# A row tile's projection in two halves of the tokens at the end of a two-layer network

## What is computed

```python
h2 = rmsnorm_2(x, norm2_g[l]) * (1.0 + scale2) + shift2
u = causal_dwconv(h2 @ w_up[l], ffn_conv_w[l], ffn_conv_b[l])
u_gate, u_val = u[..., :D_FF_2], u[..., D_FF_2:]
x = x + gate2 * ((jax.nn.silu(u_gate) * u_val) @ w_down[l])
return rmsnorm_2(x, final_g)

def rmsnorm_2(x, g):
    y = xf * lax.rsqrt(jnp.mean(xf * xf, axis=-1, keepdims=True) + EPS)
    return y * g
```

## Time and profile before

| | |
|---|---|
| median of 3 runs | 1795.24 us (1795.19 to 1796.18) |
| the profiled execution | 1792.66 us |
| its span, first to last instruction | 1790.9 us |
| PE busy | 1775.9 us, 99% of the span |
| PEld, DVE, ACT, POOL busy | 1421.8, 1041.1, 789.2, 268.5 us |
| DMA | 202.06 MB, 113 GB/s in the mean |

### The profile page before, as it was taken

The page is one execution under the profiler, slowest core; times in us unless marked ns, Lnnn a source line. Parts: engine busy times, 40 slices in busy tenths (PEclk is TensorE's granted clock), DMA queues, the critical chain, the costliest instruction groups (busy, mean ns, idle before and its releaser), DMA issues.

```text
span 1790.9 us, 20963 instructions
## 1 busy us (share of the span) xinstructions
PE 1775.9 (99%) x8086; PEld 1421.8 (79%) x8086; DVE 1041.1 (58%) x1675; ACT 789.2 (44%) x1248; POOL 268.5 (15%) x349
## 2 busy tenths in 40 slices
PE   9999999999999999999999999999999999999998
PEld 7888888878887888888887678777778788888887
DVE  8864554756566544554478796256544765435543
ACT  6554544524344222222264666356653444224443
POOL 4766536300000000000001110322210000000000
PEclk9999999999999999999999999999999999999999
DMA  6222223134344534554341422421143233233321
GB/s 218 96 87 89 71 89 92 53 114 152 94 147 164 188 141 178 209 189 153 118 135 58 132 92 76 144 66 59 36 164 95 83 94 95 94 94 94 95 94 71
DMA packets 65411, 202.06 MB, mean 113 GB/s; under 512 B 7520, under 2 KB 11872, under 8 KB 65312
## 3 DMA queue, kind: packets, MB, share of 16 engines
q1 hardware_dynamic: 65312, 200.72, 33.8%
HBM read 192.30 MB, written 8.40 MB: 112 GB/s over the span
## 4 chain that ended last, share of the span: by engine, by line
PE 94%; DVE 2%; ACT 2%; issue 0%; DMA 0%; SPq 0%; POOL 0%; ACTq 0%; DVEq 0%; POOLq 0%
PE bank L258 28%; PE bank L260 28%; PE bank L259 28%; PE bank L659 2%; PE bank L687 1%; PE bank L672 1%; PE bank L304 1%; PE bank L356 1%; PE bank L341 1%; DVE wlo L1446 1%; PE bank L537 1%; ACT whi L856 1%; PE bank L386 0%; PE bank L377 0%; PE bank L300 0%
## 5 line engine op out<-in xcount | busy, mean ns | idle before, releaser
L258 PE MATMUL bank<-tiler,whi 128*128 128x512 f32 x2260 | 912.8, 404 | 4.2 <-DVE wlo L1446 2.3
L260 PE MATMUL bank<-tiler,wlo 128*128 128x512 f32 x2260 | 892.9, 395 | 0.0
L259 PE MATMUL bank<-tiler,whi 128*128 128x512 f32 x2260 | 892.6, 395 | 0.0
L856 ACT ACTIVATE whi<-raw 128x1024 fp32r<-128x1024 f32 x284 | 298.8, 1054 | 511.6 <-PE bank L260 502.9
L258 PEld LDWEIGHTS bank<-tiler,whi 128*128 128x128 f32 x2260 | 427.1, 189 | 117.0 <-issue 16.6
L260 PEld LDWEIGHTS bank<-tiler,wlo 128*128 128x128 f32 x2260 | 426.4, 189 | 99.5
L259 PEld LDWEIGHTS bank<-tiler,whi 128*128 128x128 f32 x2260 | 426.9, 189 | 96.2 <-issue 1.7
L1446 DVE TENSOR_TENSOR wlo<-raw,whi 128x1024 fp32r<-128x1024 f32 x263 | 326.7, 1246 | 264.7 <-ACT whi L856 264.4
L2279 POOL TENSOR_TENSOR stat<-stat,scl 128x4 f32<-128x4 f32 x7 | 7.5, 1080 | 748.9 <-DVE stat L1954 428.2
L2270 POOL TENSOR_TENSOR wlo<-raw,whi 128x1024 fp32r<-128x1024 f32 x21 | 49.9, 2378 | 209.5 <-ACT whi L856 209.5
L2218 DVE SCALAR_TENSOR_TENSOR tile<-bank,sm,tile 128x511 f32<-128x511 f32 x42 | 31.5, 750 | 85.8 <-ACT tile L1410 54.1
(11 more groups left out here) (381 smaller groups left out, 1576.2 us busy)
## 6 DMA issues: line engine op xcount, KB each, us to landing
raw<-wst SPq DMA_DIRECT2D x284, 512.0 KB, 3.6
wide<-wadaT SPq DMA_DIRECT2D x52, 512.0 KB, 3.3
tile<-xT SPq DMA_DIRECT2D x16, 256.0 KB, 6.1
spare<-tile SPq DMA_DIRECT2D x16, 256.0 KB, 2.2
tile<-spare SPq DMA_DIRECT2D x16, 256.0 KB, 5.6
out<-tile SPq DMA_DIRECT2D x8, 256.0 KB, 2.5
tile<-gblk SPq DMA_DIRECT2D x5, 256.0 KB, 4.7
us<-tile SPq DMA_DIRECT2D x4, 256.0 KB, 2.0
```

Of the source, the lines that this page charges most:

```text
L258: e.matmul(bank, whi[:, o:o + 128], hi, start=start, stop=False)
L259: e.matmul(bank, whi[:, o:o + 128], lo, start=False, stop=False)
L260: e.matmul(bank, wlo[:, o:o + 128], hi, start=False, stop=stop).then_inc(*sig("blk", n))
L856: e.activation(whi[:, c % NHL * W:(c % NHL + 1) * W], raw[:, c % NRAW * W:(c % NRAW + 1) * W], ACT.Copy).then_inc(*sig("hi", c))
```

## The change

The down projection's row tile 7 of the second part is taken out of the loops. Its 11 blocks are gone through twice, first for tokens 0 to 255 (t = 0, in the bank it had), then for tokens 256 to 511 (t = 1, in bank 7), by matmuls of 256 columns. Both passes use the same blocks, so the weights' stream is the same. For each half DVE adds to the residual (`hd7`), makes the copy times the gain (`gs7`, which ACT did before), and later inverts the root and scales two banks; ACT squares, takes the root and scales two banks. Between the blocks of the second pass stand the transposes whose inputs are there and the sums of the first half. The transposed banks of j = 3 move to banks 3 and 7. The stores' order becomes 0, 4, 1, 5, 2, 6, 3, 7. Steps of chunks on ACT and DVE keep their places: the step for row tile 7 still stands behind row tile 6's on ACT.

```diff
@@ program
+        def out_bank(half_, j):
+            return B[(7 if half_ else 3) if j == 3 else j if half_ else 4 + j]
@@ tensor
-                for m in range(2, 8):
+                for m in range(2, 8 - hf):
                     proj("dn", (hf, m), bank2(p + m, "h_dn", hf, m), ACTS2, k0=11 * hf)
                 p += 8
+            n0, last_bank = count[0], bank2(p - 1, "hd7", 1)
+            count[0] += 11
+
+            def last(t, ks):
+                to = (B[7] if t else last_bank)[:, 256 * t:256 * t + 256]
+                for k in ks:
+                    n = n0 + k
+                    if t == 0:
+                        if n % CB == 0:
+                            e.wait_ge(*lo_at(n // CB))
+                        blocks[n:n + 1] = [("dn", 11 + k, 7)]
+                        first.setdefault(("dn", (1, 7)), n)
+                    o = n // CB % NHL * W + n % CB * 128
+                    hi, lo = (R(x)[:, 256 * t:256 * t + 256] for x in ACTS2[k])
+                    e.matmul(to, whi[:, o:o + 128], hi, start=k == 0, stop=False, skip_group_check=True)
+                    e.matmul(to, whi[:, o:o + 128], lo, start=False, stop=False, skip_group_check=True)
+                    ins = e.matmul(to, wlo[:, o:o + 128], hi, start=False, stop=k == 10, skip_group_check=True)
+                    if k == 10:
+                        ins.then_inc(*sig("dn7", t))
+
...
+            def half_total(t, bank):
+                e.wait_ge(*at("acc", "fin", 6))
+                for x in range(2):
+                    e.matmul(bank[:, x:x + 1], F(64)[:, 256 * t + 128 * x:256 * t + 128 * x + 128], ones[:, 0:1], start=x == 0,
+                             stop=False, skip_group_check=True)
+                e.wait_ge(*at("sq", "fin", 7, t))
+                for x in range(2):
+                    ins = e.matmul(bank[:, x:x + 1], F(66)[:, 256 * t + 128 * x:256 * t + 128 * x + 128], ones[:, 0:1],
+                                   start=False, stop=True, skip_group_check=True)
+                ins.then_inc(*sig("tot", "fin", t))
...
-            e.wait_ge(*at("h_dn", 1, 4))
-            total2("fin", 64, sums_at)
-            out_turn(0, range(4), [0, 1])
-            total3("fin", 66, sums_at)
-            out_turn(0, range(4), [2, 3])
-            out_turn(1, range(4), [4, 5, 6, 7])
...
+            def out_turn(half_, j, ms):
+                if half_ and ms[0] == 4:
+                    if j < 3:
                         e.wait_ge(*at("h_dn", 1, 4 + j))
-                        if j == 0:
-                            e.wait_ge(*at("root", "fin"))
-                    for m in ms:
+                    else:
+                        e.wait_ge(*at("hd7", 1))
+                elif j == 3:
+                    e.wait_ge(*at("hd7", 0))
+                for m in ms:
+                    if m < 7:
...
+                    else:
+                        e.wait_ge(*at("gs7", j // 2))
+                    ins = e.transpose(out_bank(half_, j)[:, m % 4 * 128:m % 4 * 128 + 128],
+                                      F(OG[m])[:, j * 128:(j + 1) * 128], ident[:, :])
+                if ms[-1] % 4 == 3:
+                    ins.then_inc(*sig("otr", half_, j))
+
+            last(0, range(11))
+            last(1, [0, 1])
+            out_turn(0, 0, [0, 1, 2, 3])
+            out_turn(0, 1, [0, 1, 2, 3])
+            last(1, [2, 3])
+            out_turn(1, 0, [4, 5, 6])
+            out_turn(1, 1, [4, 5, 6])
+            last(1, [4])
+            half_total(0, B[6])
+            last(1, [5, 6])
+            out_turn(1, 0, [7])
+            out_turn(1, 1, [7])
+            out_turn(0, 3, [0, 1, 2, 3])
+            last(1, [7, 8])
+            e.wait_ge(*at("root", "fin", 0))
+            out_turn(0, 2, [0, 1, 2, 3])
+            last(1, [9, 10])
+            out_turn(1, 2, [4, 5, 6])
+            e.wait_ge(*at("fin", 0))
+            half_total(1, B[4])
+            out_turn(1, 3, [4, 5, 6])
+            out_turn(1, 2, [7])
+            out_turn(1, 3, [7])
@@ scalar
+            e.wait_ge(*at("acc", "fin", 5))
+            for t in range(2):
+                cols = slice(256 * t, 256 * t + 256)
+                e.wait_ge(*at("hd7", t))
+                e.activation(F(66)[:, cols], F(HS[7])[:, cols], ACT.Square).then_inc(*sig("sq", "fin", 7, t))
+                e.wait_ge(*at("tot", "fin", t))
+                e.activation(stat[:, ST_F + 2 * t:ST_F + 2 * t + 2], B[4 if t else 6][:, 0:2], ACT.Sqrt, scale=1.0 / 1024,
+                             bias=scl[:, HALF + 1:HALF + 2]).then_inc(*sig("root", "fin", t))
+                e.wait_ge(*at("inv", "fin", t))
+                for j in (2 * t, 2 * t + 1):
+                    e.wait_ge(*at("otr", 1, j))
+                    e.activation(F(OT[4 + j]), out_bank(1, j), ACT.Copy, scale=stat[:, ST_F + j:ST_F + j + 1]).then_inc(
+                        *sig("fin_a", j))
@@ vector
+            for t in range(2):
+                cols = slice(256 * t, 256 * t + 256)
+                e.wait_ge(*at("dn7", t))
+                e.scalar_tensor_tensor(out=F(HS[7])[:, cols], in0=(B[7] if t else B[(p - 1) % 4])[:, cols], scalar=mod[:, 47:48],
+                                       in1=F(HS[7])[:, cols], op0=MUL, op1=ADD).then_inc(*sig("hd7", t))
+                e.wait_ge(*at("hd7", t))
+                e.tensor_scalar(F(OG[7])[:, cols], F(HS[7])[:, cols], col("gf2", 7), None, MUL).then_inc(*sig("gs7", t))
+                root_at = stat[:, ST_F + 2 * t:ST_F + 2 * t + 2]
+                e.wait_ge(*at("root", "fin", t))
+                e.reciprocal(root_at, root_at).then_inc(*sig("inv", "fin", t))
+                e.wait_ge(*at("inv", "fin", t))
+                for j in (2 * t, 2 * t + 1):
+                    e.wait_ge(*at("otr", 0, j))
+                    e.tensor_scalar(F(OT[j]), out_bank(0, j), stat[:, ST_F + j:ST_F + j + 1], None, MUL).then_inc(*sig("fin", j))
@@ sync
-            for k in (0, 1, 4, 2, 5, 3, 6, 7):
+            for k in (0, 4, 1, 5, 2, 6, 3, 7):
```

More of the change, by code:

```diff
@@ L57 @@
         "angles": "lo_a ang ang1 ang2 rel wts lru_a mod pow bpad masks",
-        "residual": "h_out h_fd h_pg h_o2 h_dn x2 inv fin",
+        "residual": "h_out h_fd h_pg h_o2 h_dn x2 inv fin hd7 gs7",
         "gated": "ap ga_ev mg fu_ev pr_ev mg2_ev mg2 ua",
@@ L821, in tensor @@
                     proj("dn", (hf, 1), bb, ACTS2, [k], 11 * hf)
-                for m in range(2, 8):
+                for m in range(2, 8 - hf):
                     proj("dn", (hf, m), bank2(p + m, "h_dn", hf, m), ACTS2, k0=11 * hf)
                 p += 8
-            def out_turn(half_, js, ms):
-                for j in js:
-                    if half_ and ms[0] == 4:
-                        e.wait_ge(*at("h_dn", 1, 4 + j))
-                        if j == 0:
-                            e.wait_ge(*at("root", "fin"))
-                    for m in ms:
-                        e.wait_ge(*at("gs", m))
[L834 to L837, removed]
@@ L839, in tensor @@
-            sums_at = B[0][:, 508:512]
-            e.wait_ge(*at("h_dn", 1, 4))
-            total2("fin", 64, sums_at)
-            out_turn(0, range(4), [0, 1])
-            total3("fin", 66, sums_at)
-            out_turn(0, range(4), [2, 3])
-            out_turn(1, range(4), [4, 5, 6, 7])
+            n0, last_bank = count[0], bank2(p - 1, "hd7", 1)
[16 more added lines that the diff above has]
+                        ins.then_inc(*sig("dn7", t))
@@ L1424, in scalar @@
                             e.activation(stat[:, 234:235], scl[:, HALF + 1:HALF + 2], ACT.Sqrt)
[L1425 to L1434, removed]
+                        if m < 7:
+                            e.wait_ge(*at("h_dn", 1, m))
+                            square("fin", m, F(HS[m]), 64, (65, 66))
+                            e.activation(F(OG[m]), F(HS[m]), ACT.Copy, scale=col("gf2", m)).then_inc(*sig("gs", m))
+            e.wait_ge(*at("acc", "fin", 5))
[11 more added lines that the diff above has]
+                        *sig("fin_a", j))
         def vector(e):
@@ L2248, in vector @@
                         add_up("fin", m - 1, 64, (65, 66))
-                    e.wait_ge(*made("dn", (hf, m)))
-                    e.scalar_tensor_tensor(out=F(HS[m]), in0=B[(p + m) % 4], scalar=mod[:, 40 + m:41 + m], in1=F(HS[m]), op0=MUL,
-                                           op1=ADD).then_inc(*sig("h_dn", hf, m))
+                    if not hf or m < 7:
+                        e.wait_ge(*made("dn", (hf, m)))
+                        e.scalar_tensor_tensor(out=F(HS[m]), in0=B[(p + m) % 4], scalar=mod[:, 40 + m:41 + m], in1=F(HS[m]),
+                                               op0=MUL, op1=ADD).then_inc(*sig("h_dn", hf, m))
                 p += 8
[L2253 to L2258, removed]
+            for t in range(2):
[12 more added lines that the diff above has]
+                    e.tensor_scalar(F(OT[j]), out_bank(0, j), stat[:, ST_F + j:ST_F + j + 1], None, MUL).then_inc(*sig("fin", j))
         def gpsimd(e):
```

## The result

| | before | changed |
|---|---|---|
| median of 19 runs | 1794.73 us | 1796.99 us |
| lowest to highest | 1792.3 to 1796.29 us | 1795.41 to 1801.5 us |
| ratio to before, 95% interval | | 1.0019 (1.0013 to 1.0025) |
| profiled execution, its span | 1792.66, 1790.9 us | 1798.92, 1796.9 us |

The medians lie 2.26 us apart; the ratio says 3.4 us (2.3 to 4.5), as do the averages of the same runs, 1794.29 and 1797.70. That is 0.19% slower, with an interval of 0.13 to 0.25%: the slowing is real, and the middle value lies within 0.2%, but the interval reaches beyond it.

A forecast was written before the change was run, and what follows sets the result against it. TensorE was taken to bound the kernel until the last row tile, then DMA bandwidth the stores. Costs of 0.25, 2.03 and 3.50 us less gains of 0.91 and 2.61 gave +2.26, 1797.5 us; range 1795.0 to 1800.2.

The forecast's parts named there:

- Part 1: Row tile 7 on TensorE: 33 matmuls become 66 of 256 columns at 0.12 us each, 0.25 us more.
- Part 3: Second half of row tile 7: 24 transposes and the first half's sums move ahead of the last matmul, 3.50 us more.
- C: Rival for row tile 7's matmuls: weight loads not hidden, 0.227 us a matmul, 1802.5 us, slower by 0.41%; chance 0.05.
- The hole: First half of row tile 7: TensorE waits at k = 7 for the last weight chunk, costing 2.03 us.
- Part 4: First half's sums, root, scalings and four stores run beside the second half's matmuls, hidden, with 1.4 us cover.
- Part 5: Second half's chain from last matmul to its first store: 2.97 us instead of 3.88, 0.91 gained.
- Part 6: Final stores: four instead of eight behind the second half's first issue, 4.72 us instead of 7.33, 2.61 gained.
- a sign that I had named for being wrong: Idle time of PE ended by ACT or DVE after 1780, from the second half meeting a late bank or scaling.
- The sum: Whole kernel: 5.78 us later end of row tile 7, less 0.91 and 2.61 gained, gives +2.26 us.
- A: Rival: TensorE's clock halves for 3.4 us behind the wait in row tile 7, +3.96 us, 1799.2 us; chance 0.33.
- B: Rival: the wait for the last chunk doesn't arise, 2.03 us less, +0.2, 1795.5 us; chance 0.10.

## Why the prediction was right, and where its chances were off

**The steps of Part 1 to Part 3.** Forecast from the tile's first matmul to the end of the last: 13.62 us (1771.85 to 1785.47) without the clock. Measured: 13.63 in the profile whose clock stayed full with an open hole, the same 13.63 with the dummy matmuls in it, 15.22 and 15.16 where the clock halved. The matmul of 256 columns was put at 0.12, it is 0.1205; the load is hidden, C is out. The hole was put at 2.03 us; the step across it is 1778.46 - 1776.38 = 2.08, of which 0.12 is the matmul's own, so 1.96, and the step behind it is 0.23 (to 1778.69) instead of 0.12: 2.07 in all. The two kernels with and without it differ by 13.63 - 11.52 = 2.11. It went away with the chunk's earlier step, came alone with the halved matmuls, and cost nothing in the kernel before: its cause is shown. The 3.50 us of moved work came out right as a sum (with the early chunk the last matmul starts 1786.85 - 1775.61 = 11.24 behind the first, less 65 steps of 0.1205 that is 3.41), not in its parts: six transposes take 0.57 (1783.89 to 1784.46), 0.095 each and not 0.111, while the first matmul behind each group takes 0.20, a cost that I didn't have. One reading was wrong without harm: what I called 14 matmuls in the earlier trace rows are 14 records of seven float32 matmuls, so the 0.111 is the distance of records, each with its load.

**Part 4.** The first early store was put at 1783.5, 11.65 behind the tile's first matmul; it is issued 1787.04 - 1775.44 = 11.60 behind it with the dummy matmuls at full clock, and 13.19 behind it in the changed kernel's profile. No idle time of TensorE shows between the hole and the tile's end, so the waits on the first half's root and scaling cost nothing, as forecast.

**Part 5 and Part 6.** From the end of the last matmul to the first store of the second half: 2.97 forecast, 1792.13 - 1789.19 = 2.94 measured. From that store to the end: 4.72 against 4.77. The chain of steps is the one that the prediction named: residual 1789.23, square 1789.75, root 1790.86, scaling 1791.36. After 1780 TensorE has one idle time ended by another engine, 0.36 us ahead of 1790.22, ended by the square. By its letter that is a sign that I had named for being wrong; but I had meant a late bank or a late scaling, and this is the wait for the square that Part 5 has in its chain.

**The sum.** +2.26 us was forecast, for the case of a full clock. Two profiles give the stretch for that case: the dummy matmuls 21.26, +2.21, and the held stores 24.13 less the 2.78 that holding them costs, 21.35, +2.30. The medians lie 2.26 apart too, but that agreement is luck: with the halved clock in the profile the stretch is +3.88, where A had +3.96, and the averages of the runs are 3.4 apart, so 2.26 lies just below the interval (2.3 to 4.5). The 0.51 between 1797.5 and the measured 1796.99 is the base alone: 1795.24 in the first three runs, 1794.73 in nineteen.

**The rivals.** A, the clock, happens: +3.88 measured where +3.96 stood. What was off is its chance. From two idle times in one profile, one with and one without a fall, I took 0.33; behind the open hole it fell in three of four. The same two idle times of the earlier trace rows in all twelve profiles say as much: near 1430 us it fell in ten, near 963 us in eight, 18 of 24. Their length, 1.81 to 1.94 us, doesn't tell which: the 1.93 of before had no fall, 1.94 with the early chunk had one. So what I gave as the forecast was, by these profiles, the rarer case, and A the usual one. The two are also not exclusive cases for a time: profiles of the same code fall into either, so the runs probably hold a mixture, and the ratio's 3.4 us lies between 2.2 and 3.9, nearer to A. How often the clock fell in the runs isn't shown: their mean clocks don't settle it, since the halves-only kernel and the early chunk both average 0.9979 over eleven executions, and only the first has the hole. With a fall in three of four the mean of the two cases is +3.5, 1798.7 on the base that I used. B did not occur, C is excluded by the step of 0.12, and the early stores do what they should.

**What I had not counted with** is that the part of the program ahead of the change varies by up to 4.4 us from one execution to the next (the tile's first matmul at 1771.85 before, at 1776.25 with the halves only). The median before moved from 1795.24 in the first three runs to 1794.73 in nineteen, and part of the changed kernel's spread has nothing to do with it. One piece of it is the clock again: behind the idle time near 963 us, which left the clock at 1.00 in the profile of before, it was halved in the profiles of eight of the ten experiments, as here in the kernel before with the early chunk:

```profile
965.20:968.60 3.40, 3.40 (x10) 2.62 (x9) 3.29 (x6) 0.00 (x0) 0.00 (x0) 0.50 0.00 0
```

Such a halving costs 1.65 us: from the end of this idle time to the end of TensorE's idle time near 1422 us are 457.84 us in the profile of before (963.81 to 1421.65) and 459.49 in that of the changed kernel with the early chunk (964.54 to 1424.03), which has it. The slower steps between 560 and 960 us at full clock are another piece, in two of the twelve profiles (changed and halves-only, 1723 matmuls instead of 1729 or 1730), whose cause I can't name.

## What to carry to other kernels

Making one engine's work finer can uncover a wait that was hidden by the coarser work: ask of each producer with a fixed place in an engine's order by how much it was early, here 0.44 us, and move it together with the consumer. Splitting the last tile moves work ahead of its end on the bound engine, and this work is paid in full; it belongs behind the last matmul, where that engine waits for the others, as far as that wait reaches. When spans of the same code differ by more than the change is worth, compare the stretch that the change touches, from a landmark ahead of it.

## What the runs showed of the hardware that I had not expected

Idle times of TensorE of 1.80 to 1.85 us inside an otherwise full stream were followed, within 2 us, by a granted clock of 0.50 (1.2 GHz) for 3.4 us in three of four profiles. Two earlier idle times of the program, 1.81 to 1.94 us long, were followed by such a fall in 18 of 24 cases. In the one profile with matmuls of unused results in the hole there was no fall, and the stretch was 1.67 us shorter. The first matmul behind a group of transposes takes 0.20 us to the next, against 0.12 in the stream.
